# Initial normalization of a two-layer encoder kernel: the first weight chunk is split by ScalarE and VectorE instead of GpSimd, and the small constants are made at the end of the stage

## What is computed

```python
h = jnp.concatenate([meta, x], axis=1)
h = layer_norm(h, emb_ln_g, emb_ln_b)            # the initial normalization
lb_all = jnp.cumsum(softmax(c_lb_logits, axis=0), axis=0) - ...   # bounds of group C's gates
for l in range(DEPTH):
    # inside mixer_layer:
    h_in = x @ w_in                                # projections
    lam = exp(sum(lp[0] * lp[1])) - exp(sum(lp[2] * lp[3])) + lam_init    # used by group B only
    f = lb_h + (1.0 - lb_h) * sigmoid(z)           # gates of group C: the bounds are used here
    ...
    h = layer_norm(ALPHA * h + y, ln_g[l], ln_b[l])
```

## Time and profile before

| | |
|---|---|
| median of 3 runs | 1951.52 us (1950.04 to 1954.15) |
| the profiled execution, its own time | 1951.07 us |
| its span in the trace | 1949.8 us |
| TensorE busy in the span | 1741.2 us (89%) |
| VectorE busy | 1143.0 us (59%) |
| ScalarE busy | 886.3 us (45%) |
| GpSimd busy | 405.2 us (21%) |

### The profile page before, as it was taken

The page is one execution under the profiler, slowest core; times in us unless marked ns, Lnnn a source line. Parts: engine busy times, 40 slices in busy tenths (PEclk is TensorE's granted clock), DMA queues, the critical chain, the costliest instruction groups (busy, mean ns, idle before and its releaser), DMA issues. The chain is left out here.

```text
span 1949.8 us, 37518 instructions
## 1 busy us (share of the span) xinstructions
PE 1741.2 (89%) x14474; PEld 1621.5 (83%) x14474; DVE 1143.0 (59%) x2793; ACT 886.3 (45%) x2700; POOL 405.2 (21%) x390
## 2 busy tenths in 40 slices
PE   3899999999889998978999989999998898988796
PEld 3798998999788787857988989989998787876696
DVE  6475584345457777874175845833554576767615
ACT  4434544345425665663053444452452354656603
POOL 5430221210121001020454203113103001012044
PEclk9899999999989999999999999999998899999998
DMA  7200100100110000032122001011001000003312
GB/s 248 63 26 12 55 23 27 51 25 10 34 45 6 28 10 28 17 130 94 44 95 70 23 12 55 23 32 46 28 10 52 23 9 28 30 8 106 111 62 87
DMA packets 98192, 91.89 MB, mean 47 GB/s; under 512 B 6176, under 2 KB 88336, under 8 KB 98016
## 3 DMA queue, kind: packets, MB, share of 16 engines
q1 hardware_dynamic: 98016, 89.49, 14.1%
HBM read 68.30 MB, written 21.17 MB: 46 GB/s over the span
## 5 line engine op out<-in xcount | busy, mean ns | idle before, releaser
L798 PE MATMUL psum<-w_hi,hT_hi 128*128 128x256 f32 x2400 | 704.0, 293 | 24.3 <-DVE rb L1687 13.7
L798 PE MATMUL psum<-w_hi,hT_lo 128*128 128x256 f32 x2400 | 681.8, 284 | 0.0
L798 PE MATMUL psum<-w_lo,hT_hi 128*128 128x256 f32 x2400 | 681.3, 284 | 0.0
L798 PEld LDWEIGHTS psum<-w_hi,hT_hi 128*128 128x128 f32 x2400 | 459.8, 192 | 36.0 <-DVE rb L1687 16.7
L798 PEld LDWEIGHTS psum<-w_hi,hT_lo 128*128 128x128 f32 x2400 | 459.7, 192 | 0.0
L798 PEld LDWEIGHTS psum<-w_lo,hT_hi 128*128 128x128 f32 x2400 | 459.1, 191 | 0.0
L760 POOL CAST w_hi<-w_raw 128x512 fp32r<-128x512 f32 (+1 forms) x168 | 110.2, 656 | 1377.7 <-DMA w_raw<-in_w_in 813.2
L764 POOL TENSOR_TENSOR w_lo<-w_raw,w_hi 128x512 fp32r<-128x512 f32 (+1 forms) x168 | 211.7, 1260 | 30.9 <-DVE neg_max L1827 19.4
L1826 DVE TENSOR_REDUCE row_max<-psum 128x1 f32<-128x1024 f32 x136 | 165.4, 1216 | 33.7 <-PE psum L938 33.5
L1087 PE MATMUL psum<-vg_b,aT_b 128*128 128x128 f32 (+1 forms) x1224 | 159.4, 283 | 23.3 <-ACT aT_b L1387 23.3
L1087 PEld LDWEIGHTS psum<-vg_b,aT_b 128*128 128x128 f32 (+1 forms) x1224 | 145.3, 189 | 32.2 <-ACT aT_b L1387 28.6
(11 more groups left out here) (161 smaller groups left out, 2677.8 us busy)
## 6 DMA issues: line engine op xcount, KB each, us to landing
w_raw<-in_w_in SPq DMA_DIRECT2D x104, 256.0 KB, 3.7
h_dram<-hbuf SPq DMA_DIRECT2D x16, 512.0 KB, 2.6
w_raw<-in_w_out SPq DMA_DIRECT2D x16, 512.0 KB, 4.1
hbuf<-h_dram SPq DMA_DIRECT2D x16, 512.0 KB, 5.5
qk_b<-y_dram SPq DMA_DIRECT2D x16, 512.0 KB, 3.3
y_dram<-y_stage SPq DMA_DIRECT2D x96, 64.0 KB, 1.6
w_raw<-in_w_in SPq DMA_DIRECT2D x12, 512.0 KB, 4.5
hbuf<-in_x SPq DMA_DIRECT2D x8, 512.0 KB, 7.3
```

Of the source, the lines that this page charges most:

```text
L798: last = nc.tensor.matmul(out_ap, lhs[a](k), rhs[b](k), start=k == 0 and a + b == 0, stop=k == KT - 1 and b == 1)
```

## The change

SP issues the rows first, the first weight chunk behind tile 2 instead of tile 3, and the set-up's five small transfers behind the second chunk. ScalarE makes the `hi` of the first chunk, two pieces behind the normalization of tile 3 and two behind that of tile 4 (`first_hi`); VectorE makes the `lo` behind its gain of tiles 3 and 4 (`first_lo`). GpSimd adds the biases of tiles 0 to 4, then alternates: bias of tile 5, piece 0 of chunk "b", bias of 6, piece 1, bias of 7, piece 2, bias of 8, piece 3. The set-up runs on VectorE and ScalarE behind everything of tile 8 (h6 included) and ahead of the clipping of U0 to U2.

```diff
+FIRST_SPLIT = {3: (0, 1), 4: (2, 3)}
...
+        for t in range(REAL):
+            sp.dma_start(hbuf[:, t], x[0, t * P:(t + 1) * P, :]).then_inc(rows_in[t], 16)
+            if t == 0:
+                sp.dma_start(ident[:], eye).then_inc(ident_in, 16)
+                load_ln(emb_ln_g, emb_ln_b)
+            if t == 2:
+                load_chunk(0, "C0", "qf")
+        sp.dma_start(hbuf[0:META, MT], meta).then_inc(rows_in[MT], 16)
+        load_chunk(0, "C0", "b")
         sp.dma_start(lam_sb[:], b_lam.partition_broadcast(P)).then_inc(setup_in, 16)
         for l in range(DEPTH):
             for p in range(2):
                 sp.dma_start(lbl[:, l, p:p + 1],
...
-            if t == 3:
-                load_chunk(0, "C0", "qf")
...
-        add_ln_bias("I", range(2))
-        split_chunk(0, "C0", "qf")
-        add_ln_bias("I", range(2, 7))
-        split_chunk(0, "C0", "b")
-        add_ln_bias("I", range(7, TILES))
+        add_ln_bias("I", range(5))
+        for j in range(W_PIECES):
+            add_ln_bias("I", [5 + j])
+
+            pool.wait_ge(w_split, W_PIECES)
+            split_piece(0, "C0", "b", j)
...
+        def first_hi(pieces):
+            for j in pieces:
+                ks = slice(j * PIECE, (j + 1) * PIECE)
+                act.wait_ge(w_loaded[0][j * W_LOADS // W_PIECES], 16 * loads_before(0))
+                nc.scalar.copy(w_hi[:, 0, ks, :], w_raw[:, 0, ks, :]).then_inc(w_hi_done, 1)
...
-        act.wait_ge(setup_v, 1)
-        then(nc.scalar.activation(lam_exp[:], lam_dot[:], ACT.Exp))
-        nc.scalar.activation(lbl[:], lbl[:], ACT.Exp).then_inc(setup_s, 1)
...
                 for t in range(TILES):
                     rstd_of("I", t)
+                    if t in FIRST_SPLIT:
+                        first_hi(FIRST_SPLIT[t])
                     for u in START_AFTER[t]:
...
+                act.wait_ge(setup_v, 1)
+                then(nc.scalar.activation(lam_exp[:], lam_dot[:], ACT.Exp))
+                nc.scalar.activation(lbl[:], lbl[:], ACT.Exp).then_inc(setup_s, 1)
                 for u in START_AFTER[TILES]:
...
+        def first_lo(pieces):
+            for j in pieces:
+                ks = slice(j * PIECE, (j + 1) * PIECE)
+                dve.wait_ge(w_hi_done, j + 1)
+                tt(w_lo[:, 0, ks, :], w_raw[:, 0, ks, :], w_hi[:, 0, ks, :].bitcast(F32), ALU.subtract).then_inc(w_split, 1)
...
                     ln_apply("I", t)
+                    if t in FIRST_SPLIT:
+                        first_lo(FIRST_SPLIT[t])
                     for u in START_AFTER[t]:
                         if u[0] == "h":
                             lo_of_rows("h", 0, u[1])
+                setup()
                 for u in [u for t in range(TILES) for u in START_AFTER[t] if u[0] != "h"]:
                     gate_bound((0, *u))
                     pending.append((0, *u))
```

More of the change, by code:

```diff
@@ L671, in _ @@
                              c_lb_logits[l, p * P:(p + 1) * P].rearrange("(p o) -> p o", o=1)).then_inc(setup_in, 16)
[L672 to L676, removed]
-            if t == 3:
-                load_chunk(0, "C0", "qf")
-        sp.dma_start(hbuf[0:META, MT], meta).then_inc(rows_in[MT], 16)
-        load_chunk(0, "C0", "b")
         for dst, src in ((pair_sb[:], pair_mask), (cos_sb[:], rope_cos), (sin_sb[:], rope_sin),
@@ L743, in beside_maximum, with split_piece, split_chunk @@
                 pool.wait_ge(b_max, B_COMP[l, *step, 0])
-        def split_chunk(l, g, name, head=None):
+        def split_piece(l, g, name, j, head=None):
             i = CHUNK[l, g, name]
             n = sum(p[1] for p in CHUNKS[i][3])
-            for j in range(W_PIECES):
[L749 to L764, removed]
+            ks = slice(j * PIECE, (j + 1) * PIECE)
+            raw, hi, lo = (w[:, i % 2, ks, 0:n] for w in (w_raw, w_hi, w_lo))
+            pool.wait_ge(w_loaded[i % 2][j * W_LOADS // W_PIECES], 16 * loads_before(i))
+            if head:
+                beside_maximum(l, head, j, 0)
+            if g == "O" and j:
+                pool.wait_ge(norm_w_in, 16)
+                pool.tensor_tensor(raw, raw, view(norm_w, 0, P, l * 6 + (j - 1) * PIECE, [[1, PIECE], [0, n]]),
+                                   ALU.mult).then_inc(w_scaled, 1)
+                pool.wait_ge(w_scaled, (W_PIECES - 1) * (l * (DM // CW) + name) + j)
+            pool.tensor_copy(hi, raw).then_inc(w_hi_done, 1)
+            pool.wait_ge(w_hi_done, W_PIECES * i + j + 1)
+            if head:
+                beside_maximum(l, head, j, 1)
+            pool.tensor_tensor(lo, raw, hi.bitcast(F32), ALU.subtract).then_inc(w_split, 1)
+        def split_chunk(l, g, name, head=None):
+            for j in range(W_PIECES):
+                split_piece(l, g, name, j, head)
         def add_ln_bias(l, tiles):
@@ L1564, in _ @@
         nc.vector.memset(one_c[:], 1.0)
[L1565 to L1582, removed]
@@ L1583, in _, with setup @@
-        then(tt(lb[:, 0], lbl[:, 0], lbl[:, 0], ALU.subtract))
-        then(ts(one_lb[:], lb[:], -1.0, 1.0, ALU.mult, ALU.add))
+        def setup():
+            dve.wait_ge(setup_in, 16 * (1 + 2 * DEPTH))
+            for l in range(DEPTH):
+                for i in range(2):
+                    then(nc.vector.tensor_tensor_reduce(lam_tmp[:], lam_sb[:, l, 2 * i, :], lam_sb[:, l, 2 * i + 1, :],
+                                                        1.0, 0.0, ALU.mult, ALU.add, lam_dot[:, l, i:i + 1]))
+            then(tt(lb_max[:], lbl[:, 0], lbl[:, 1], ALU.max))
+            for l in range(DEPTH):
+                then(tt(lbl[:, l], lbl[:, l], lb_max[:], ALU.subtract))
+            dve.sem_inc(setup_v, 1)
+            dve.wait_ge(setup_s, 1)
+            for l in range(DEPTH):
+                then(stt(neg_lam[:, l:l + 1], lam_exp[:, l, 1:2], -LAM_INIT[l], lam_exp[:, l, 0:1], ALU.add, ALU.subtract))
+            then(tt(lb_sum[:], lbl[:, 0], lbl[:, 1], ALU.add))
+            then(nc.vector.reciprocal(lb_sum[:], lb_sum[:]))
+            for l in range(DEPTH):
+                then(tt(lbl[:, l], lbl[:, l], lb_sum[:], ALU.mult))
+            then(tt(lb[:, 1], lbl[:, 0], lbl[:, 1], ALU.add))
+            then(tt(lb[:, 1], lb[:, 1], lbl[:, 0], ALU.subtract))
+            then(tt(lb[:, 0], lbl[:, 0], lbl[:, 0], ALU.subtract))
+            then(ts(one_lb[:], lb[:], -1.0, 1.0, ALU.mult, ALU.add))
```

## The result

The changed kernel is slower: median 1955.92 us of 13 runs (1954.23 to 1963.83), the kernel before 1951.52 of 13 (1946.89 to 1955.23). The ratio is 1.0031, 95% interval 1.0020 to 1.0042, that is +6.0 us (3.9 to 8.2). Timed again with the last experiments it was 1.0027 (1.0014 to 1.0039). The forecast had the right sign and a time inside its range, but it said +2.85 us, less than half of what was measured, and gave 0.7 to "no measurable change".

What follows compares the result with a forecast made beforehand. It took the chain of small steps in front of TensorE to bound the first stage; U0's -1.75 and the set-up's +4.6 gave +2.85 us on 1951.07, 1953.9, stated as 1954.0, range 1949.5 to 1957.0.

Steps and rivals of the forecast that it cites:

- no measurable change: Whole kernel: the case that the time stays within about 0.2% (3.9 us) of the kernel before; chance 0.70.
- The rows earlier: Start: five issues leave the head of SP's queue, so rows and tile 1 land 2.32 us earlier.
- VectorE's lo halves and the port: First chunk: GpSimd's biases 3 and 4 are let in before pieces 1 and 3, 2.3 us each.
- The rival in which VectorE keeps the port: First chunk: no bias let in between VectorE's lo pieces; U0 -6.1, sum -1.5, 1949.6 us; chance 0.15.
- ScalarE's casts: First chunk: four casts from SBUF, estimated at 0.61 us each, add nothing to the time.
- U0, -1.75 expected: First chunk: U0 starts at 36.75 instead of 38.52, and the rest moves with it.
- Set-up, +4.6 expected: Behind tile 8: 4.11 us of set-up plus 2.1 of waits beside GpSimd make U5 start 4.6 us later.
- The sum, +2.85: Whole kernel: U0's -1.75 and the set-up's +4.6 added, giving 1953.9, stated as 1954.0 us.
- the term for the clock: TensorE after standstills: the sum had nothing for slow matmuls; they appeared only as a rival, chance 0.16.
- The clock rival as it was written: TensorE after standstills: all three slow stretches become 6.1 us long, 2.3 us more, 1956.2 us; slow side's chance 0.16.
- The chances: Whole kernel, against a 3.9 us threshold: slower 0.23, same 0.70, faster 0.07.

Runs made afterwards that it cites:

- e4: Changed kernel with the set-up placed as in e3 and VectorE's lo halves ahead of the gains of tiles 3 and 4; ratio 0.9969 to the kernel before.
- e2: Kernel before with only the set-up and its transfers moved to where the change puts them, behind tile 8 and chunk b; ratio 1.0011 to the kernel before.
- e10: The changed kernel run again, unaltered; ratio 1.0027 to the kernel before.
- e1: Changed kernel with the set-up, its transfers and ScalarE's two exponentials back at the very front; ratio 0.9999 to the kernel before.
- e3: Changed kernel with the set-up under U0, between the statistics of tile 6 and the gain of tile 5; ratio 0.9990 to the kernel before.
- e5: Changed kernel with only the lo halves moved ahead of the gains of tiles 3 and 4, set-up still behind tile 8; ratio 1.0010 to the kernel before.
- e7: Changed kernel with set-up and the gates of U0 to U4 behind hi and lo of h8; ratio 0.9974 to the kernel before.
- e8: Changed kernel with GpSimd's pieces 1 to 3 of chunk b one bias earlier each; single time 1959.98 us.
- e6: Kernel before with the rows' transfers issued first and the set-up placed as in e3, no split moved; ratio 0.9995 to the kernel before.
- e9: e4 plus the gates of U0 to U4 behind lo of h8 as in e7; ratio 0.9957 to the kernel before, median 1943.9 us.

## Why the prediction came out as it did

- **The rows earlier, -2.32 expected:** 1.73 measured in the first profile (tile 1's statistics at 11.61, not 11.0). Over the ten profiles with the rows first they start between 10.77 and 11.84, 11.4 in the mean: the landing itself spreads by 1 us. This term was too large by 0.4 in the mean.
- **VectorE's lo halves and the port:** right. 3.45 and 3.44 us for a pair, pieces 1 and 3 behind a bias addition. The rival in which VectorE keeps the port is ruled out, and e4 shows what it would have given: U0 at 33.2 (the prediction says 32.4; its own terms add up to 32.6). The Trainium skill's rule in "SBUF — State Buffer" (who interferes with whom) that the port is an exclusive lock, and whoever comes second waits for the other's whole instruction, agrees with these rows, and with the dot product's 1.41 us, which no row of before had shown.
- **ScalarE's casts:** 1.12 for two that overlap, 0.60 to 0.61 for one, as the prediction's estimate of 0.61 had it, and hidden as said.
- **U0, -1.75 expected:** -1.25 measured, the missing 0.5 being tile 1's late landing. Only -0.50 was left behind U2, because TensorE's pace rose when it had before. I had carried U0's gain through to U5 as if that pace didn't change, and in this profile 0.75 of it was lost. In e2 and e10 it went the other way: U2 started 2.8 us earlier than before. Over all twelve profiles U0's start and U2's are 16.7 to 18.4 us apart, so this looks like the scatter of single executions and not like a loss that belongs to the change.
- **Set-up, +4.6 expected:** the standstill grew by 4.36. Right in place, in mechanism and in the length of the standstill; e1, e2, e3, e5 and e7 each show it, e8 its port part.
- **The sum, +2.85, and the step that failed:** by U0 and the standstill alone (-1.25 + 4.36) it is +3.1, by U5 +3.8, by the timings +6.0 and +5.3. The step that failed is the term for the clock: the sum put it at nothing and took the standstill to cost its length; the clock was only a rival with 0.16. The record puts more on it in two ways.
  - *Timings.* Three pairs of kernels differ only in where the set-up stands, under U0 or behind tile 8: e3 and the changed kernel, e4 and e5, e6 and e2. The ratios differ by 0.0041, 0.0041 and 0.0016, that is 8.0, 8.0 and 3.1 us, each uncertain by some 3 us. The standstills differ by 4.35, 4.38 and 3.73. So a set-up at the end costs 6.4 us in the mean, 2.2 more than the standstill it makes.
  - *Traces.* From U5's start to the first COPY_PREDICATED the five kernels with a standstill of 6.4 to 7.0 us take 32.8 to 33.6 us, 33.1 in the mean. The five with 2.6 us take 30.5 to 33.1, 31.6 in the mean, and the two with 0.87 take 28.5 and 29.0. All five long ones have a slow stretch of 4.5 to 5.6 us behind U5 and a second one behind the start of the vg product, where the granted clock is 0.56 to 0.67. Of the five short ones the kernel before and e3 have both; e1, e4 and e6 have 2.7 to 3.0 us behind U5 and none at the vg product.

  That is 1.5 us for the clock, and the sum becomes +4.6, inside the intervals of both timings. It also puts e5 at +0.5 (measured +2.0, -0.4 to +4.5), e2 at +3.3 (+2.1, -0.2 to +4.5) and, with the 2.8 us less of a short standstill, e7 and e9 inside theirs. It remains five single executions against five whose ranges touch, so the size of the clock's share is supported and not settled, and about 1 us is open. The one profile of before that the prediction was built on took 33.07 us, the longest of its group, so it could not show that a kernel with a 2.6 us standstill often gets by with less.
- **The clock rival as it was written** (all three slow stretches of the earlier trace rows 6.1 us long) did not come true: they were 4.8, 5.6 and 5.2 us. Its time of 1956.2 is near the measured one in part by luck.
- **The chances** were wrong with it: a centre of 2.85 with a clock rival of up to +2.3 made "slower by over 3.9" more likely than the 0.23 given.

## What to carry to other kernels

Work that is taken off the first engine in a chain pays only where that engine is still the last to arrive; here VectorE took over the wait. A standstill of TensorE can cost more than its length, since slow matmuls may follow it; look at several executions before you put that at nothing. A short piece of set-up is free under a transfer or a running product and costs its full length, and the other engine's instructions beside it, in front of the operand that TensorE waits for; look at what is queued behind it, not at how late it is. Two-input VectorE instructions that follow a release of GpSimd let GpSimd in between them (3.45 us for a pair of lo halves, against 1.24): issue them before the release.

## What the runs showed of the hardware that was not expected

A dot product over 64 columns (0.23 us alone) lasted 1.41 to 1.43 us beside a bias addition on GpSimd. The granted clock of TensorE was 1.00 behind a standstill of 0.87 us before U5 (e7, e9; matmuls 0.16 apart at once) and 0.50 behind 2.63 us (e3; 0.29 apart). How long it stayed there differed between executions: 2.7 to 6.2 us behind a standstill of 2.6 us. The same program's U5 moved by 2.75 us between two executions whose standstills before U2 and U5 agreed to 0.02 us; 0.67 of it came from tile 1's landing.
